# Two 64-slot units side by side per expert step, in plain float32 products

## The reference

```python
def run(args):                       # one block of tokens of one expert e
    xblk, e = args
    return (jax.nn.silu(xblk @ w_gate[e]) * (xblk @ w_up[e])) @ w_down[e]
y = jnp.einsum('nkd,nk->nd', y_pairs, gate)          # two experts per token
h = layer_norm(DN_ALPHA * h + y)
```

## Time and profile before

| what | value |
|---|---|
| three runs | 2576.66, 2580.95, 2582.27 us; median 2580.95 |
| span of the profiled execution | 2577.0 us; the profile gives nothing around it |
| PE, PEld, DVE, ACT, POOL busy | 94%, 81%, 79%, 65%, 25% of the span |
| granted TensorE clock, mean | 0.970 of full |
| bytes moved by DMA | 565.81 MB, mean 220 GB/s |

### The profile page before, as it was taken

One profiled execution on the slowest core, in us unless ns is written; L12 is line 12 of the kernel. 1 busy time (PEld: TensorE's weight loads), 2 busy tenths in 40 slices (PEclk: granted clock), 3 DMA queues, 4 the chain that ended last, 5 costly groups with the idle time before them and its releaser, 6 DMA issues. The chain is left out here.

```text
span 2577.0 us, 37706 instructions
## 1 busy us (share of the span) xinstructions
PE 2426.1 (94%) x12715; PEld 2077.8 (81%) x12715; DVE 2025.5 (79%) x2589; ACT 1683.3 (65%) x1814; POOL 653.5 (25%) x480
## 2 busy tenths in 40 slices
PE   9989998987979999999999599999979999999997
PEld 8979978885867888888888499997867888888885
DVE  4788876777889989999898544547779998998887
ACT  3369836666227788887887466663147888877775
POOL 0105814343002222222221412121013222223232
PEclk9999999997989999999999699999989999999999
DMA  5502354324349699988998411114259699999995
GB/s 181 134 13 87 83 99 128 105 67 136 101 148 405 228 346 375 366 322 316 320 376 290 173 58 36 39 34 159 94 204 356 234 353 369 376 370 363 376 373 191
DMA packets 121902, 565.81 MB, mean 220 GB/s; under 512 B 24119, under 2 KB 32567, under 8 KB 72528
## 3 DMA queue, kind: packets, MB, share of 16 engines
q1 hardware_dynamic: 96688, 513.25, 55.1%
q0 software_dynamic: 25120, 51.36, 7.2%
HBM read 575.32 MB, written 73.28 MB: 252 GB/s over the span
## 5 line engine op out<-in xcount | busy, mean ns | idle before, releaser
L2218 DVE TENSOR_TENSOR e0wlo<-e0raw,e0whi 128x2048 fp32r<-128x2048 f32 x214 | 487.1, 2290 | 59.8 <-ACT e0whi L2066 59.8
L2066 ACT ACTIVATE e0whi<-e0raw 128x2048 fp32r<-128x2048 f32 x214 | 409.9, 1915 | 90.3 <-PE e0banks L94 78.2
L2218 DVE TENSOR_TENSOR e1wlo<-e1raw,e1whi 128x2048 fp32r<-128x2048 f32 x138 | 313.2, 2286 | 43.4 <-ACT e1whi L2066 43.2
L2066 ACT ACTIVATE e1whi<-e1raw 128x2048 fp32r<-128x2048 f32 x138 | 263.9, 1913 | 40.0 <-PE e1banks L94 33.5
L92 PE MATMUL e0banks<-e0whi,e0xh 128*128 128x512 f32 x576 | 231.1, 401 | 2.9 <-DVE e0xl L2223 2.7
L94 PE MATMUL e0banks<-e0whi,e0xl 128*128 128x512 f32 x576 | 226.1, 392 | 0.0
L93 PE MATMUL e0banks<-e0wlo,e0xh 128*128 128x512 f32 x576 | 225.6, 392 | 0.0
L2218 DVE TENSOR_TENSOR e_wu<-e1raw,e_wu 128x2048 fp32r<-128x2048 f32 x70 | 160.2, 2290 | 17.8 <-ACT e_wu L2066 17.7
L92 PE MATMUL odd_banks<-h2T_hi,odd_w_hi 128*128 128x348 f32 x480 | 171.6, 357 | 0.8 <-DVE h2T_lo L2539 0.5
L2066 ACT ACTIVATE e_wu<-e1raw 128x2048 fp32r<-128x2048 f32 x70 | 134.2, 1918 | 50.4 <-PE e1banks L94 30.7
L93 PE MATMUL odd_banks<-h2T_lo,odd_w_hi 128*128 128x348 f32 x480 | 155.1, 323 | 0.0
(11 more groups left out here) (526 smaller groups left out, 6898.2 us busy)
## 6 DMA issues: line engine op xcount, KB each, us to landing
e0raw<-in_moe_w_gate SPq DMA_DIRECT2D x72, 1024.0 KB
e0raw<-in_moe_w_up SPq DMA_DIRECT2D x72, 1024.0 KB
e0raw<-in_moe_w_down SPq DMA_DIRECT2D x72, 1024.0 KB
e1raw<-in_moe_w_gate SPq DMA_DIRECT2D x70, 1024.0 KB
e1raw<-in_moe_w_up SPq DMA_DIRECT2D x70, 1024.0 KB
e1raw<-in_moe_w_down SPq DMA_DIRECT2D x70, 1024.0 KB
qki_w_raw<-in_w_even SPq DMA_DIRECT2D x22, 512.0 KB, 5.8
pre<-in_conv_band SPq DMA_DIRECT2D x32, 320.0 KB, 3.0
```

What stands on the lines that cost most here:

```text
L2066: act.activation(w_hi[i], raw[:, i, :], ACT.Copy).then_inc(hi_done[i], 1)
L2218: dve.tensor_tensor(w_lo[i], raw[:, i, :], w_hi[i].bitcast(F32), ALU.subtract).then_inc(lo_done[i], 1)
```

## The change

Slots are rounded up to units of 64. By the counts above that makes 49 units in layer 0 and 50 in layer 1. The list of units is cut in two halves of 25; step ("column") g works on unit g of the first half and unit g+25 of the second at once: rows 0 to 63 of every tile belong to the one, rows 64 to 127 to the other. Each half has a full set of six chunk buffers (12 MiB in all). The splits into high and low are gone: `both` gives TensorE, for each 128 rows of the contraction, one plain float32 matmul with 64 slots into PSUM partitions 0 to 63 and one, with other weights, into 64 to 127. x and the hidden tile are copied once out of PSUM. A chunk buffer is reloaded when the products of the column before have used it (`used`). The scatter of a column is two indirect DMAs, one after the other, each with the indices of one half (those of the other half are out of bounds).

Experts new to each column, over both halves, by the counts above: layer 0: 2 0 2 0 2 1 1 1 0 2 1 0 1 1 1 2 2 1 2 2 2 2 1 2 1; layer 1: 2 0 1 2 2 1 2 0 2 1 2 1 1 1 1 0 1 1 2 1 1 2 2 2 1.

The core of the diff:

```diff
-MAXB = -(-(2 * T + NE * (P - 1)) // P)
+UNIT = P // 2
+MAXU = (2 * T + NE * (UNIT - 1)) // UNIT
+MAXC = -(-MAXU // 2)
...
-SUM_CHUNKS, GAIN_CHUNK = (2, 3, 4, 5, 0), 1
+SUM_CHUNKS, GAIN_CHUNK = (2, 3, 8, 9, 4), 5
...
             def reload(chunks, g):
-                e = sp.value_load(meta_i[0:1, bass.ds(g + E_AT, 1)], min_val=0, max_val=NE - 1)
-                new = sp.value_load(meta_i[0:1, bass.ds(g + R_AT, 1)], min_val=0, max_val=1)
+                e = [expert_of(u) for u in (g, g + half)]
+                new = [sp.value_load(meta_i[0:1, bass.ds(u + R_AT, 1)], min_val=0, max_val=1) for u in (g, g + half)]
                 for i in chunks:
-                    sp.wait_ge(lo_done[i], g)
-                    load(i, e, new)
-
-            for i in FIRST_LOADS:
-                load(i, 0)
-            sp.wait_ge(x_in, 16)
-            load(WU[1], 0)
-            m = blocks_but_two(sp)
+                    sp.wait_ge(used[i], g)
+                    for s in range(2):
+                        load(i, s, e[s], new[s])
+
+            for i in range(NCH):
+                load(i, 0, 0)
+            m = columns_but_two(sp)
+            half = sp.snap(sp.value_load(meta_i[0:1, H_AT:H_AT + 1], min_val=NE // 2, max_val=MAXC))
+            e = expert_of(half)
+            for i in range(NCH):
+                load(i, 1, e)
...
-                pool.indirect_dma_start(sum_d, bass.IndirectOffsetOnAxis(sx[:, 0:1].bitcast(U32), 0), y[:], None,
-                                        bounds_check=n_tok - 1, oob_is_err=False, compute_op=ALU.add).then_inc(y_stored, 16)
-                pool.wait_ge(y_stored, g * 16 + 16)
-                pool.sem_inc(y_free, 1)
+                for s in range(2):
+                    pool.indirect_dma_start(sum_d, bass.IndirectOffsetOnAxis(sx[:, s:s + 1].bitcast(U32), 0), rows[:], None,
+                                            bounds_check=n_tok - 1, oob_is_err=False, compute_op=ALU.add).then_inc(y_stored[s], 16)
+                    pool.wait_ge(y_stored[s], stored)
+                    pool.sem_inc((y_half, y_free)[s], 1)
...
             def turn(g):
-                split_h(g)
-                for i in WG:
-                    split_w(i, g + 2)
+                take_h(g)
                 silu(g + 1)
-                for i in WU:
-                    split_w(i, g + 2)
-                split_x(g + 2)
-                split_w(4, g + 1)
+                take_x(g + 2)
                 take_y(g)
-                split_w(5, g + 1)
...
+                link(dve.tensor_scalar(half_i[:], pend[:, NE - 1:NE], 1.0, None, ALU.add))
+                link(dve.tensor_scalar(half_i[:], half_i[:], 1, None, ALU.arith_shift_right))
+                link(dve.tensor_scalar(half_f[:], half_i[:], float(UNIT), None, ALU.mult))
...
             def turn(g):
-                split_h(g)
-                for i in WG:
-                    split_w(i, g + 2)
-                split_w(2, g + 2)
                 hidden(g + 1)
-                split_w(3, g + 2)
-                split_x(g + 2)
-                for i in WD:
-                    split_w(i, g + 1)
+                take_x(g + 2)
...
+            def both(out, stat, chunk, a, start, stop):
+
+                for s in range(2):
+                    last = pe.matmul(out[HALF[s], :], stat[:, HALF[s]], raw[NCH * s + chunk][:, a], start=start, stop=stop)
+                return last
+
+            def weights_of(i, g):
+                for s in range(2):
+                    pe.wait_ge(landed[NCH * s + i], g * 16 + 16)
...
             def up(i, g):
                 ps = (g_ps, u_ps)[i // 2]
-                pe.wait_ge(lo_done[i], g + 1)
+                if i < 2:
+                    pe.wait_ge((xt_first, xt_second)[i], g + 1)
+                weights_of(i, g)
                 for k in range(4 * (i % 2), 4 * (i % 2) + 4):
-                    a = slice((k % 4) * FE, (k % 4 + 1) * FE)
-                    last = mm3(pe, ps[:], (x_hi[:, k, :], x_lo[:, k, :]), (w_hi[i][:, a], w_lo[i][:, a]),
-                               k == 0, k == KC - 1)
+                    last = both(ps, xt[:, k, :], i, slice((k % 4) * FE, (k % 4 + 1) * FE), k == 0, k == KC - 1)
                 last.then_inc(used[i], 1)
```

More of the change, by code:

```diff
@@ L1861, in rows @@
     def rows(self, n):
-        return self.raw[0:toks(self.blocks[n]), SUM_CHUNKS[n // 2], (n % 2) * D:(n % 2) * D + D]
+        return self.raw[0:toks(self.blocks[n]), KEPT_CHUNKS.index(SUM_CHUNKS[n // 2]), (n % 2) * D:(n % 2) * D + D]
     def gain(self, j):
-        return self.raw[:, GAIN_CHUNK, j * D:(j + 1) * D]
+        return self.raw[:, KEPT_CHUNKS.index(GAIN_CHUNK), j * D:(j + 1) * D]
     def load_gains(self, sp):
@@ L1875, in load_rows, with experts @@
             sp.dma_start(self.rows(n), self.sum_d[at:at + toks(b), :]).then_inc(self.loaded[n], 16)
-def experts(nc, name, const, picks, h_d, sum_d, wg_d, wu_d, wd_d, first, raw, sums, rest=None):
-    CH, NCH = EXPERT_CHUNK, EXPERT_CHUNKS
+def experts(nc, name, const, picks, h_d, sum_d, wg_d, wu_d, wd_d, first, kept_raw, sums, rest=None):
+    NCH = EXPERT_CHUNKS
     nb = NB - first
@@ L1884, in experts @@
     n_tok = T if first == 0 else SEQ
+    HALF = (slice(0, UNIT), slice(UNIT, P))
     with Ctx(nc) as c:
[L1886 to L1899, removed]
+        own_chunks = [i for i in range(2 * NCH) if i not in KEPT_CHUNKS]
+        own_raw = c.sb(name + "own", [P, len(own_chunks), EXPERT_CHUNK])
+        raw = [kept_raw[:, KEPT_CHUNKS.index(i), :] if i in KEPT_CHUNKS else own_raw[:, own_chunks.index(i), :] for i in range(2 * NCH)]
+        x, xt = c.sb(name + "x", [P, D]), c.sb(name + "xt", [P, KC, P])
+        sg, hid, ht = c.sb(name + "sg", [P, FE]), c.sb(name + "hid", [P, FE]), c.sb(name + "ht", [P, FE // P, P])
         y = c.sb(name + "y", [P, D])
-        ix, sx = c.sb(name + "ix", [P, 1], I32), c.sb(name + "sx", [P, 1], I32)
+        ix, sx = c.sb(name + "ix", [P, 1], I32), c.sb(name + "sx", [P, 2], I32)
         tok_f, tok_n, gate2 = c.sb(name + "_tf", [P, 2]), c.sb(name + "_tn", [P, 2, NB - 1]), c.sb(name + "_g2", [P, 2])
@@ L2401, in slots @@
             def slots(j, b, start, stop):
-                pe.matmul(ht_ps[:, 0:MAXB], is_l[:, j, b, :], in_b[:, j, b, :], start=start, stop=False)
-                return pe.matmul(ht_ps[:, 0:MAXB], is_h[:, j, b, :], in_b[:, j, b, :], start=False, stop=stop)
+                for table, opens, ends in ((is_l, start, False), (is_h, False, stop)):
+                    for s in range(2):
+                        last = pe.matmul(ht_ps[HALF[s], 0:MAXC], table[:, j, b, :], in_b[:, j, b, s, :], start=opens, stop=ends)
+                return last
             for j in range(2):
@@ L2428, in _ @@
                 for b in range(first, NB):
-                    last = pe.matmul(y_ps[:, 0, 0:MAXB], is_pf[:, j, b, :], is_g[:, j, b, :], start=j == 0 and b == first,
-                                     stop=j == 1 and b == NB - 1)
+                    for s in range(2):
+                        last = pe.matmul(y_ps[HALF[s], 0, 0:MAXC], is_pf[:, j, b, :], is_g[:, j, b, s, :], start=j == 0 and b == first,
+                                         stop=j == 1 and b == NB - 1)
             last.then_inc(by_slot_mm, 1)
```

302 lines of the change are left out of this document (108 added, 194 removed).

## The result

The changed kernel takes 2551.05 us (median; before it 2579.9 in the same comparison), a ratio of **0.9887, 95% interval 0.9867 to 0.9906**: 29 us less, where 12 were forecast. The median takes in one of the four executions that was slow as a whole (3350.43 us at a granted clock of 0.65), the ratio leaves it out. The profiled execution has a span of 2545.9 us against 2577.0.

The account below looks back on a forecast made before the run. TensorE sets the pace, with little lead over the loads. Layer 0: 575 + 57 + 6 against 651; layer 1: 575 + 47 + 6 against 637; route +2, end +8: -12 us, 2569 us; range 2465 to 2650.

Parts of the forecast that it names:

- the walk: Expert loads, column by column: 14.8 us per new expert plus 4, stalls above 12 us backlog; 57 and 47 us.
- Start: First product of each layer: needs both halves' first chunks, so begins at 779 instead of 773, +6 us a layer.
- route: Routing in each layer: some eight more small VectorE operations and half-wide tables, +1 us a layer.
- the end of layer 0: Last y to reading the sums: four scatters in sequence, 22 us instead of 14.2, +8 us.
- the column: TensorE's work per column: products 20.5 us, transposes 0.8 and 0.4, group ends 1.3; 23.0 us, 575 for 25.
- The load stalls of layer 1: TensorE waiting for expert loads in layer 1: stalls of 10, 7, 6, 2, 11, 11, together 47 us.
- The end of layer 1: Rows wait for an earlier column's scatter while TensorE has a column and a down left: hidden, no cost.
- Halves don't overlap: Rival, every step: the two half-array products run one after the other, column 42.2 us, about 3437 us; chance 0.14.
- Scatter loop: Rival, GpSimd's round with two landings: 24 to 26 us against 23.0, costs 40 us, 2609; chance 0.09.
- Loads never bind: Rival, expert loads: backlog is worked off better, only 575 + 6 us a layer is left, 2465; chance 0.14.
- Mode changes: Rival, each column: six changes between whole and half array cost 1.0 us, 28 us in light columns, 2597; chance 0.06.
- Clock: Rival, heavy columns: TensorE at half clock, 17 columns lose up to 9 us each, up to 2720; chance 0.05.

Follow-up runs that it names:

- run with whole-array products: Against the changed kernel, each pair of half-array products became one whole-array product with the first half's weights, second half's experts left out: turns 21.93 us, span 2539.4 us.
- gain-load run: Against the changed kernel, the gain and bias loads at the end of layer 1 were issued between row loads 4 and 5: ratio 0.9847 to the kernel before.

## Why the prediction was right or wrong

**What held.** The halves work together, the load queue is the new bound, the stalls of layer 0 sit about where the walk puts them and are as large: 58 us measured, 57 forecast. Walked again, it has 10, 7, 11, 11, 11, 7 us in columns 16, 18, 19, 20, 21 and 23; the turns 16 to 23 are 3.0, 4.1, 9.5, 4.2, 9.6, 10.3, 1.8 and 8.0 us over 22.6, and turn 4, where the walk has none, 6.5. Start, route and the end of layer 0 came within 1.5 us of the forecast. The direction was right, the size was not: 31 us of span instead of 12.

**The term that was mis-sized: the column.** "Three groups of products stand between transposes ... (0.43 us a group): 1.3." There are two groups: down of one block and the gate chunk of the next follow each other, with no transposes between. They cost 0.65 us together, not 1.3, and not for the reason given: no half works alone at their ends (run with whole-array products). The other terms were a little short: 24 steps are 20.6 us, not 20.5, and the transposes 1.3, not 1.2. So a column is 20.6 + 1.3 + 0.65 = 22.6 us, as measured, not 23.0, and without stalls the stages took 567 and 566 us, not 575: 17 of the 19 us that were missing. In layer 1 three more terms were off, and nearly cancel: load stalls 17 us smaller, late gathers of 7.5 us and an end of 6 us.

**The load stalls of layer 1** were some 30 us, not 47, and late gathers added 7.5. The heavy column is cheaper than the 34 us of the walk: its turns took 31 to 33 us. The 4 us that the walk took for gather and scatter are too much. Between 1190 and 1310 us 47.05 MB of weights arrive, 2.67 us a chunk and 32.1 us for 12; 12 chunks at the forecast's 2.47 are 29.6, which leaves 2.5 us, and to leave out one scatter changed no heavy turn. Layer 0 came out right all the same because two things cancel: cheaper columns, but also stalls at the start (turn 4) and the clock, which the sum left out.

**The end of layer 1** was costed at nothing, "hidden". It cost 6 us. The scatter was as early as forecast, it landed 9 us ahead of TensorE's last product; what was missed was the queue behind it. SyncE waits for that scatter (until 2497.6) before it issues eight row loads and only then the two loads of gain and bias, for which ScalarE stood. Moved, they gave 4.7 us back.

**The start** was right in its sum, +6, and half right in its cause: the second half's chunk was the last to come, but TensorE had already stood 4 us for the gather of x, which took 8.8 us instead of some 4 before. The granted clock was 0.50 for 10.2 us from 774.0 on; with the loads reordered alone there were 3.4 and 6.8 us at 0.50, with filler products in the gap as well it stayed at 1.00. The reordering gave 3 and 4 us, not 7 to 9.

**The rivals.** *Halves don't overlap*: false as the kernel is written, but it comes partly true with another order of issue (33.0 us a turn). *Scatter loop*: true in part, and missing from the sum. Landings have a median of 9.4 us, about the 9.2 at which it was to decide, and ScalarE waits 88 and 149 us for `y_free`. From 2300 us on in layer 1 the rounds take 25 us, as this rival has it; the slack holds for a few turns, then x is late twice and the layer loses 7.5 us. In layer 0 TensorE never waits for it in the turns, but the loop sets the end of that layer. The rival's 40 us were 7.5, and the two runs with shorter rounds (one scatter, no reloads) have no late x. *Loads never bind*: false; without reloads the stages are 95 us shorter. *Mode changes*: a column has four changes between whole and half array, not six, and they cost 0.65 us with the group ends. As the halves start together there and whole-array groups pay nothing for their ends, this cost stands in place of the 1.3 us of the sum, not beside it. The rule of the Trainium skill (TensorEngine Tiling, Key Properties) is that a change of mode drains the engine. The traces agree as far as they go: the seams take 0.09 us more ahead of transposes and 0.20 to 0.26 behind them than with whole-array products, and no run here shows what happens within. *Clock*: mean 0.96 against 0.970; behind the waits there are stretches of 3.4 and 6.8 us at 0.50, 20 us in layer 0 and 17 in layer 1; a loss of 19 us at most, half of their length, far from the 140 of that rival.

Three numbers of the rivals are off by little: 3437 us counts the later start twice (12 us), the changes of mode are four a column, and the lists have 19 columns with two new experts behind the first, not 17.

**What stays open**: what TensorE does at a seam, why turn 4 differs by 4.6 us between executions of the same code, why a chunk at the start of a nearly empty queue takes 6.5 us to its product, and half of the difference between the gain-load run and the change.

## What to carry to other kernels

When a change makes the loads the bound, further savings on the engine are worth almost nothing: 33 us less products moved the stages by 9 us, 15 us less by none. What then pays is the order of the loads (20 us in the stage) and what stands in line at the ends of the stage (5 us and 3 to 4 each), and none of these shows in the busy shares. An engine that is busy for 22% of the span can still be late (GpSimd's loop, 2.8 us longer a round than the turn beside it, ate its lead), so look at rounds and not at shares. And before a per-turn price is summed, count in the trace how often a turn has it: one group too many, at 0.43 us, is 21 us over 50 columns.

## What the runs showed of the hardware

- How far half-array products overlap depends on the order of issue: with 1, 4 and 8 products of a half in a row (8 in gate and up alone) a turn took 22.6, 26.6 and 33.0 us, and in the last two the other half started four records ahead of its turn. That is, a product can start before one of the other half that was issued earlier. The Trainium skill (TensorEngine Tiling, Key Properties) says that different tiles can execute in parallel; the pairs 0.01 us apart agree, and these runs add that the order of issue decides how much of it happens.
- A wait of TensorE for weights can be followed by a stretch at half clock. In the change, at turn 4:

```profile
873.65 3.60 PE L2225 MATMUL e0banks<-e0raw,e0xt 128*64 128x512 f32 x16
880.59 6.63 PE L2225 MATMUL e0banks<-e0raw,e0xt 128*64 128x512 f32 x16 [3.34 <-DMA e0raw<-in_moe_w_up]
```

  After 3.34 us of waiting the same 16 records take 6.63 us instead of 3.60. This wait costs twice. Shorter gaps can do it too: one of 2.33 us at 1235.8 was followed by 3.4 us at 0.50. Filler products in the idle gap at the start kept the clock up.
- The HBM figure of a profile is no measure of what was moved. The run without reloads moved 196.61 MB by DMA, and the page of its profile says:

```profile
HBM read 733.65 MB, written 86.39 MB: 338 GB/s over the span
```

  The change, which moved 569.94 MB, has 746.75 there. It seems to count loads that are issued and skipped.
